# Attention loop of a hybrid encoder block on one Trainium2 core: transposes, mixture and scores of three different units placed together, the twelve projection products behind them

## Chip, cores, metric

One core of one Trainium2 chip. The time is that of one launch of the whole kernel in microseconds, the median of three runs. A profiled execution of the same kernel gives the trace.

## What is computed

The reference is one encoder layer on x (1, 512, 1024) in float32: a token mixer with two branches, a residual with layer norm, and a mixture of experts. Only the second branch of the mixer and the projections beside it matter here:

```python
q, k: (S, 8 heads, 2, 64)    v: (S, 8 heads, 128)
scores = q k^T / 8, masked to chunks of 64 tokens, for each head and each of its 2 parts
p = softmax(scores);  attn = p[part 0] - lam * p[part 1];  o = attn @ v
yb = rms_norm(o) * subln_g * (1 - lam_init)
merged = sigmoid(h @ w_gr) * (ya @ p_rnn) + sigmoid(h @ w_ga) * (yb @ p_attn)
mixer  = merged @ w_out
```

Afterwards 64 experts of width 256 are routed (8 of them per token), and each result row is scattered into a table `y_rows` in HBM that has been cleared to zero before.

## The kernel before, in words

The kernel is written engine by engine; each engine has its own program, in order, and they meet at semaphores. Each waits with `wait_ge`. TensorE (PE) multiplies and transposes, ScalarE (ACT) and VectorE (DVE) read the PSUM banks, GpSimd (POOL) does small things, SyncE (SP) issues DMAs.

**Units.** The attention stage walks over 32 units `u = 4 h + i`: head `h` (8) and block `i` (4) of 128 queries. Unit u sees `i + 1` key tiles of 128. Its steps are:
- `scores(u)` (L996, matmuls at L1007): eight recorded matmuls on 64x64 tiles into banks 2 and 3, or 4 and 5. It waits for the exponentials of u-2.
- `maxima(u)` (DVE, L1927 and L1929), the two exponentials (ACT, L1498), `combine(u)` (DVE, L1935 to L1940), which gives `attn`.
- `transpose_attn(u)` (L1011, L1018): i+1 transposes into bank 6, which ACT copies to `attn_t` (L1491). It waits for `attn` of u, for the copy of u-1, and, where u is the first unit of a head from head 2 on, at L1016 for `ybt_ready`, the semaphore of the head output (below), because that uses bank 6 too.
- `mix_values(u)` (L1021, L1031): `attn_t` times v, 2(i+1) recorded matmuls into bank 7, which DVE copies to `yb` (L1974).

**Heads.** When four units of a head are done, POOL squares `yb` (L734), DVE averages (`head_mean`, L1955), POOL takes the inverse root (L736), DVE scales (`head_norm`, L1961), PE transposes the four tiles into bank 6 (`transpose_head`, L1035, L1041), ACT reads bank 6 as `yb_t` (L1480, `ybt_ready`) and rounds it to `yb_hi` (L1482), DVE forms `yb_lo` (`head_low`, L1966).

**Products.** Beside the attention the stage computes the groups ("gr", h) and ("pr", h), 24 products each, twelve products to a unit: 128x128 weights times 128x512 data, in lines L900, L901 and L902 (the operands are split in a high and a low part, so each k takes three products). Weights arrive by DMA in blocks of two groups (L544), are rounded by ACT (`split_hi`, L1361) and the rest is formed by DVE (`split_lo`, L1745, `wlo_ready`); `begin` makes PE wait for that. Twice a head the bank is read: `gate_out` (ACT, L1417) and `merge_first` (DVE, L1950).

**The order** is written out by hand. PE in iteration u: scores(u), six products, transposes of u-1, six products, mixture of u-1, and at the first unit of a head from h = 2 on `transpose_head(h-2)`. One more iteration at the end serves unit 31, beside the 24 products of ("ga", 0). ACT in iteration u: copy of the transposes of u-1, exponentials of u, head output, weights. DVE: copy of the mixture of u-2, combine of u-1, maxima of u, then merge, weights, head steps.

**The zeros.** SP clears `y_rows` in eight transfers of 2 MB (L564) between the weight blocks, from `zeros`, a [128, 1024] tile written by POOL (L727).

Of the kernel before, what the change touches and what calls it, by code (L numbers as in the profile page):

```python
# [21 lines left out]
ACT = mybir.ActivationFunctionType  # L22
AX = mybir.AxisListType

P = 128
T = 512
D = 1024
NT = T // P
KD = D // P
NH = 8  # L30
# [91 lines left out]
def hybrid_block(nc, x, c, w_ada, b_ada, w_in, conv_w, conv_b, lru_w_a, lru_b_a, lru_w_i, lru_b_i, lru_lambda,  # L122
# [3 lines left out]
    with ctx:  # L126
# [74 lines left out]
        attn = [at(f"attn{p}", 198 + 2 * p, [P, T]) for p in range(2)]  # L201
        attn_t = at("attn_t", 202, [P, T])
        gate_s = at("gate_s", 206, [P, T])
# [95 lines left out]
        y_all = [at(f"y_all{s}", 38 + 16 * s, [P, TOPK // 2, D]) for s in range(4)]  # L299
        zeros = at("zeros", 170, [P, D])  # L300
        lane = at("lane", 201, [P, P])
# [213 lines left out]
        def _(sp):  # L515
# [22 lines left out]
            for n, (kind, b) in enumerate(BLOCKS):  # L538
# [20 lines left out]
                if kind in ("gr", "pr") and (kind, b) != ("gr", 0):  # L559

                    part = 2 * b + (kind == "pr")
                    sp.wait_ge(zeros_ready, 1)
                    for clear in ((0, 1) if part == 1 else (part,)):
                        sp.dma_start(y_rows[clear * T:(clear + 1) * T, :].rearrange("(j p) d -> p j d", p=P),  # L564
                                     bcast(zeros[:, :], 1, NT)).then_inc(rows_zeroed, 16)
                if (kind, b) == ("ga", 3):
# [274 lines left out]
        def _(pe):  # L841
# [179 lines left out]
            def mix_values(u):  # L1021
# [8 lines left out]
                for j in range(i + 1):  # L1030
                    last = nc.tensor.matmul(bank[7][:, 0:P], attn_t[:, j * P:(j + 1) * P], v_s[:, j, h * P:(h + 1) * P],  # L1031
                                            start=(j == 0), stop=(j == i))
                last.then_inc(mixed, 1)

            def transpose_head(h):  # L1035

                pe.wait_ge(yb_ready, h + 1)
                if h >= 1:
                    pe.wait_ge(ybt_ready, h)
                for t in range(NT):  # L1040
                    last = nc.tensor.transpose(bank[6][:, t * P:(t + 1) * P], yb[:, t, h * P:(h + 1) * P], ident[:, :])  # L1041
                last.then_inc(yb_tr, 1)

            for b in range(2):
                pe.wait_ge(main_read[b], 5 * KD // 2)
            for u in range(NT * NH + 1):
                h, i = u // NT, u % NT
                if u < NT * NH:
                    scores(u)
# [3 lines left out]
                    if u == 2:  # L1053
                        pe.wait_ge(yalo_ready, KD)
                    first, middle, end = (4 * (i % 2) + n for n in (0, 2, 4))
                    moving = (h_hi, h_lo) if i < 2 else (ya_hi, ya_lo)
                    channel_major(group, range(first, middle), *moving)
                else:
                    begin(("ga", 0))
                    channel_major(("ga", 0), range(KD // 2))  # L1060
                if u >= 1:
                    transpose_attn(u - 1)
                if u < NT * NH:
                    channel_major(group, range(middle, end), *moving)
                else:
                    channel_major(("ga", 0), range(KD // 2, KD))
                if u >= 1:
                    mix_values(u - 1)
                if u >= 2 * NT and i == 0:
                    transpose_head(h - 2)  # L1070

            begin(("pa", 0))
# [277 lines left out]
        def _(act):  # L1350
# [132 lines left out]

            for u in range(NT * NH + 1):
                h, i = u // NT, u % NT
                if u >= 1:
                    act.wait_ge(attn_tr, u)
                    if u >= 2:
                        act.wait_ge(mixed, u - 1)
                    w = ((u - 1) % NT + 1) * P  # L1490
                    nc.scalar.activation(attn_t[:, 0:w], bank[6][:, 0:w], ACT.Copy).then_inc(attn_t_ready, 1)  # L1491
                if u < NT * NH:
# [4 lines left out]
                    for k in range(2):  # L1497
                        nc.scalar.activation(prob[u % 2][k][:, 0:(i + 1) * P], bank[2 + 2 * (u % 2) + k][:, T - (i + 1) * P:T],  # L1498
                                             ACT.Exp, bias=unit_stats[:, u % 2, 2 + k:3 + k], scale=HC ** -0.5,
                                             accum_out=unit_stats[:, u % 2, 4 + k:5 + k]).then_inc(prob_ready, 1)  # L1500
                if u >= 2 * NT and i == 0:
                    head_out(h - 2)
# [169 lines left out]
        def _(dve):  # L1672
# [295 lines left out]

            for u in range(NT * NH + 2):
                h, i = u // NT, u % NT  # L1970
                if u >= 2:
                    ph, pi = (u - 2) // NT, (u - 2) % NT
                    dve.wait_ge(mixed, u - 1)
                    V.tensor_copy(yb[:, pi, ph * P:(ph + 1) * P], bank[7][:, 0:P]).then_inc(mixed_read, 1)  # L1974
                if 1 <= u <= NT * NH:
                    combine(u - 1)
                if u < NT * NH:
                    maxima(u)
                if i == 0 and h >= 1:
                    merge_first(h - 1)  # L1980
                if u == NT * NH:
                    split_lo(GROUP[("pa", 0)])
                if i == 1 and u < NT * NH:
                    split_lo(GROUP[("pr", h)])
                if i == 3 and u < NT * NH:
                    split_lo(GROUP[("gr", h)] + 2)
                if i == 1 and h >= 2:
                    head_low(h - 2)
                if i == 2 and h >= 1:
                    head_mean(h - 1)  # L1990
                if i == 3 and h >= 1:
                    head_norm(h - 1)

# [520 lines left out]
```

## Time and profile before

| | |
|---|---|
| median of 3 runs | 1302.7 us (1301.36 to 1304.47) |
| the profiled execution's own time | 1302.48 us |
| its span, first to last instruction | 1300.8 us |
| mean granted TensorE clock | 0.993 |
| PE busy | 1261.6 us (97%) |
| DVE busy | 837.4 us (64%) |
| ACT busy | 740.1 us (57%) |
| attention stage, first scores to last transposes | about 282 to 434 us |

Matmuls are pipelined, and a row shows one for longer than the distance to the next (a product takes 0.39 us in its row and the next begins 0.23 us later). So PE's busy share hides short waits, and what a step costs is read from the distance between starts. In a row of the timeline "x8" means that eight instructions of the same line follow each other; the row's second number is from the first's start to the last's end.

### The profile page before, as it was taken

Reading aid. Unit: us, or ns where it says so; the run is one execution under the profiler, and the core shown is the slowest. Engines: PE = TensorE matmul, PEld = TensorE weight load, DVE = VectorE, ACT = ScalarE, POOL = GpSimd, SP = SyncE. Lnnn points to the kernel's source line nnn. Section 1 sums busy time; section 2 is a strip of 40 time slices with the busy share of each in tenths; the row PEclk is TensorE's granted clock in tenths of the full one; section 3 lists DMA queues with packets and bytes.
Section 4 is the critical chain, followed back from the end, with each engine's and each line's share of the span. In section 5 each row is a group of like instructions: output and inputs, shape, how many; then the busy total and the mean of one; then the engine's idle time right before and its main releaser. Section 6 shows DMA issues by size and latency. Waiting matters only on the chain.

```text
span 1300.8 us, 22921 instructions
## 1 busy us (share of the span) xinstructions
PE 1261.6 (97%) x6367; PEld 725.4 (56%) x6367; DVE 837.4 (64%) x1771; ACT 740.1 (57%) x968; POOL 192.0 (15%) x373
## 2 busy tenths in 40 slices
PE   6999999999999999989999999999999999999995
PEld 6777788877777788865433333333333333333342
DVE  5837777667878555897455565555455555555578
ACT  4356452334554423113577777777677777777721
POOL 1000000000010100132122212221221221222100
PEclk9999999999999999999999999999999999999998
DMA  8832446669832551454789899999999999998396
GB/s 319 253 96 89 140 154 219 210 244 184 284 101 62 180 209 58 161 228 170 314 320 383 335 413 403 391 381 370 385 363 400 390 417 377 397 402 324 112 387 252
DMA packets 111603, 353.69 MB, mean 272 GB/s; under 512 B 20518, under 2 KB 59543, under 8 KB 85826
## 3 DMA queue, kind: packets, MB, share of 16 engines
q1 hardware_dynamic: 92642, 303.05, 63.6%
q0 software_dynamic: 18912, 50.01, 10.7%
q8 instruction: 28, 0.46, 0.2%
q14 instruction: 21, 0.17, 0.0%
HBM read 326.08 MB, written 47.21 MB: 287 GB/s over the span
## 4 chain that ended last, share of the span: by engine, by line
PE 79%; DVE 9%; DMA 7%; SPq 2%; issue 1%; ACT 1%; POOL 0%; ACTq 0%; DVEq 0%
PE bank L1244 25%; PE bank L1269 12%; PE bank L900 9%; PE bank L902 9%; PE bank L901 9%; DMA gu<-in_we_up 4%; PE bank L1231 3%; PE bank L1007 2%; PE bank L1254 2%; PE bank L1031 1%; DMA y_all<-y_rows 1%; PE bank L1133 1%; SPq L534 1%; DMA ada_first<-in_w_ada 1%; DVE x L2415 1%
## 5 line engine op out<-in xcount | busy, mean ns | idle before, releaser
L1244 PE MATMUL bank<-gu_use,x_t 128*64 128x512 f32 x1664 | 369.9, 597 | 0.0
L1595 ACT ACTIVATE gu_use<-gu 128x1024 f32 x208 | 209.1, 1058 | 57.3 <-PE bank L1244 32.4
L1244 PEld LDWEIGHTS bank<-gu_use,x_t 128*64 128x64 f32 x1664 | 115.2, 137 | 217.6 <-issue 217.4
L1588 ACT ACTIVATE down_use<-down 128x2048 f32 x103 | 190.9, 1901 | 0.0
L1269 PE MATMUL bank<-down_use,act_t 128*64 128x512 f32 x832 | 187.4, 592 | 0.0
L900 PE MATMUL bank<-h_hi,w_lo 128*128 128x512 f32 x432 | 173.9, 402 | 1.4 <-DVE w_lo L1745 1.4
L902 PE MATMUL bank<-h_hi,w_hi 128*128 128x512 f32 x432 | 168.7, 391 | 0.0
L2273 DVE COPY gu_use<-gu 128x1024 f32 x208 | 133.1, 691 | 55.3 <-PE bank L1244 41.8
L901 PE MATMUL bank<-h_lo,w_hi 128*128 128x512 f32 x432 | 168.4, 390 | 0.0
L1745 DVE TENSOR_TENSOR w_lo<-stream,w_hi 128x1024 fp32r<-128x1024 f32 x72 | 87.9, 1221 | 96.7 <-ACT w_hi L1361 96.6
L2239 DVE TENSOR_TENSOR pick<-slot_id,places 128x512 bf16<-128x512 f32 x53 | 36.7, 692 | 145.4 <-POOL columns L808 145.4
L1269 PEld LDWEIGHTS bank<-down_use,act_t 128*64 128x64 f32 x832 | 59.6, 137 | 119.0 <-issue 119.0
L787 POOL DMA_INDIRECT x_rows<-u_rows,row_index x52 | 53.6, 1032 | 434.5 <-DVE row_index L2251 252.4
L900 PEld LDWEIGHTS bank<-h_hi,w_lo 128*128 128x128 f32 x432 | 81.1, 188 | 28.1 <-issue 12.3
L1361 ACT ACTIVATE w_hi<-stream 128x1024 fp32r<-128x1024 f32 x72 | 75.9, 1055 | 32.1 <-PE bank L902 25.9
L902 PEld LDWEIGHTS bank<-h_hi,w_hi 128*128 128x128 f32 x432 | 81.1, 188 | 17.7
L901 PEld LDWEIGHTS bank<-h_lo,w_hi 128*128 128x128 f32 x432 | 81.2, 188 | 15.3
L2305 DVE TENSOR_TENSOR y_item<-bank,g_row 128x512 f32<-128x512 f32 x104 | 67.0, 686 | 2.9 <-PE bank L1269 2.1
L2251 DVE TENSOR_SCALAR row_index<-bank 64x1 int32<-64x1 f32 x104 | 23.4, 225 | 63.4 <-PE bank L1222 62.7
L1612 ACT ACTIVATE x_t<-bank 128x512 f32<-128x512 f32 x104 | 56.2, 598 | 4.1 <-PE bank L1231 4.1
L796 POOL DMA_INDIRECT y_rows<-y_item,y_index x50 | 50.2, 1005 | 43.4 <-issue 33.3
L1231 PE MATMUL bank<-ident,x_rows 128*128 128x128 f32 x416 | 55.8, 277 | 0.3 <-ACT x_t L1612 0.2
(345 smaller groups left out, 1721.6 us busy)
## 6 DMA issues: line engine op xcount, KB each, us to landing
gu<-in_we_gate SPq DMA_DIRECT2D x64, 1024.0 KB
gu<-in_we_up SPq DMA_DIRECT2D x64, 1024.0 KB
down<-in_we_down SPq DMA_DIRECT2D x64, 1024.0 KB
stream<-in_w_in SPq DMA_DIRECT2D x28, 1024.0 KB, 7.4
ada_w<-in_w_ada POOLq DMA_DIRECT2D x8, 2048.0 KB, 9.7
y_rows<-zeros SPq DMA_DIRECT2D x8, 2048.0 KB, 13.8
y_all<-y_rows SPq DMA_DIRECT2D x7, 2048.0 KB, 15.4
ada_first<-in_w_ada SPq DMA_DIRECT2D x16, 512.0 KB, 11.2
```

The source lines that it names most:

```text
L900: nc.tensor.matmul(o, w_lo[s][:, k, :], hi[:, k, :], start=(k == 0), stop=False)
L901: nc.tensor.matmul(o, w_hi[s][:, k, :], lo[:, k, :], start=False, stop=False)
L902: last = nc.tensor.matmul(o, w_hi[s][:, k, :], hi[:, k, :], start=False, stop=(k == KD - 1))
L1231: last = nc.tensor.transpose(bank[2 + k // 4][:, k % 4 * P:(k % 4 + 1) * P], x_rows[item.par][:, k * P:(k + 1) * P], ident[:, :])
L1244: last = nc.tensor.matmul(bank[item.par][rows, :], x_t[:, k, rows], gu_use[h][:, :, k, :], start=(k == 0), stop=(k == KD - 1))
L1269: last = nc.tensor.matmul(bank[5 + half][rows, :], act_t[:, f, rows], down_use[h][:, f, cols], start=(f == 0), stop=(f == FE - 1))
L1361: nc.scalar.activation(w_hi[n % 2][:, :, :], stream_of(group), ACT.Copy).then_inc(whi_ready, 1)
L1588: nc.scalar.activation(down_use[h][:, :, :], down[:, bass.ds(slot, 1), :, :].rearrange("p o k n -> p (o k) n"), ACT.Copy).then_inc(down_ta ...
L1595: return nc.scalar.activation(gu_use[h][:, 1, ks, :], gu[:, bass.ds(slot, 1), 1, ks, :].rearrange("p o k n -> p (o k) n"), ACT.Copy)
L1745: V.tensor_tensor(w_lo[n % 2][:, :, :], stream_of(group), w_hi[n % 2][:, :, :].bitcast(F32), ALU.subtract).then_inc(wlo_ready, 1)
L2273: return V.tensor_copy(gu_use[h][:, 0, ks, :], gu[:, bass.ds(slot, 1), 0, ks, :].rearrange("p o k n -> p (o k) n"))
L2305: last = V.tensor_tensor(y_item[item.par][:, cols], bank[5 + half][:, :], g2_row[:, cols], ALU.mult)
```

## The change

On PE, iteration u becomes: transposes of u-2, mixture of u-3, scores of u, all twelve products; then, at the second unit of a head, `transpose_head(h-2)`, with a new wait for the copies of the transposes before it. There are 34 iterations instead of 33, with the 24 products of ("ga", 0) shared out over the last two, and the mixture of unit 31 stands behind the loop. ACT and DVE follow: the copy is that of u-2, the head output moves to the second unit of the head, the `yb` copy is that of u-3 and comes after `combine(u-1)`, `head_low`, `head_mean` and `head_norm` move one unit on. `attn_t` gets a second buffer. It takes 2 KB of the place that `zeros` had, so `zeros` is [128, 512] now and each of the eight clearing transfers writes 2 KB runs instead of 4 KB runs, in another order of rows.

```diff
@@ -199,7 +199,7 @@
 
         prob = [[at(f"prob{p}{k}", 190 + 4 * p + 2 * k, [P, T]) for k in range(2)] for p in range(2)]
         attn = [at(f"attn{p}", 198 + 2 * p, [P, T]) for p in range(2)]
-        attn_t = at("attn_t", 202, [P, T])
+        attn_t = [at("attn_t0", 172, [P, T]), at("attn_t1", 202, [P, T])]
         gate_s = at("gate_s", 206, [P, T])
 
         branch = at("branch", 198, [P, T])
@@ -297,7 +297,7 @@
         shared_early = at("shared_early", 118, [P, FE, D])
 
         y_all = [at(f"y_all{s}", 38 + 16 * s, [P, TOPK // 2, D]) for s in range(4)]
-        zeros = at("zeros", 170, [P, D])
+        zeros = at("zeros", 170, [P, D // 2])
         lane = at("lane", 201, [P, P])
         tail_sums = at("tail_sums", 201.5625, [P, 2 * NT])
         passed = at("passed", 106, [P, D])
@@ -561,8 +561,8 @@
                     part = 2 * b + (kind == "pr")
                     sp.wait_ge(zeros_ready, 1)
                     for clear in ((0, 1) if part == 1 else (part,)):
-                        sp.dma_start(y_rows[clear * T:(clear + 1) * T, :].rearrange("(j p) d -> p j d", p=P),
-                                     bcast(zeros[:, :], 1, NT)).then_inc(rows_zeroed, 16)
+                        rows = y_rows[clear * T:(clear + 1) * T, :].rearrange("(p j) (c d) -> p (j c) d", p=P, c=2)
+                        sp.dma_start(rows, bcast(zeros[:, :], 1, 2 * NT)).then_inc(rows_zeroed, 16)
                 if (kind, b) == ("ga", 3):
 
                     sp.wait_ge(main_done, GROUP[("pr", KD - 1)] + 1)
@@ -1028,13 +1028,14 @@
                 else:
                     pe.wait_ge(ada_ready, 2)
                 for j in range(i + 1):
-                    last = nc.tensor.matmul(bank[7][:, 0:P], attn_t[:, j * P:(j + 1) * P], v_s[:, j, h * P:(h + 1) * P],
+                    last = nc.tensor.matmul(bank[7][:, 0:P], attn_t[u % 2][:, j * P:(j + 1) * P], v_s[:, j, h * P:(h + 1) * P],
                                             start=(j == 0), stop=(j == i))
                 last.then_inc(mixed, 1)
 
             def transpose_head(h):
 
                 pe.wait_ge(yb_ready, h + 1)
+                pe.wait_ge(attn_t_ready, min((h + 2) * NT, NT * NH))
                 if h >= 1:
                     pe.wait_ge(ybt_ready, h)
                 for t in range(NT):
@@ -1043,8 +1044,12 @@
 
             for b in range(2):
                 pe.wait_ge(main_read[b], 5 * KD // 2)
-            for u in range(NT * NH + 1):
+            for u in range(NT * NH + 2):
                 h, i = u // NT, u % NT
+                if u >= 2:
+                    transpose_attn(u - 2)
+                if u >= 3:
+                    mix_values(u - 3)
                 if u < NT * NH:
                     scores(u)
                     group = ("gr" if i < 2 else "pr", h)
@@ -1052,22 +1057,15 @@
                         begin(group)
                     if u == 2:
                         pe.wait_ge(yalo_ready, KD)
-                    first, middle, end = (4 * (i % 2) + n for n in (0, 2, 4))
                     moving = (h_hi, h_lo) if i < 2 else (ya_hi, ya_lo)
-                    channel_major(group, range(first, middle), *moving)
+                    channel_major(group, range(4 * (i % 2), 4 * (i % 2) + 4), *moving)
                 else:
-                    begin(("ga", 0))
-                    channel_major(("ga", 0), range(KD // 2))
-                if u >= 1:
-                    transpose_attn(u - 1)
-                if u < NT * NH:
-                    channel_major(group, range(middle, end), *moving)
-                else:
-                    channel_major(("ga", 0), range(KD // 2, KD))
-                if u >= 1:
-                    mix_values(u - 1)
-                if u >= 2 * NT and i == 0:
+                    if i == 0:
+                        begin(("ga", 0))
+                    channel_major(("ga", 0), range(4 * i, 4 * i + 4))
+                if h >= 2 and i == 1:
                     transpose_head(h - 2)
+            mix_values(NT * NH - 1)
 
             begin(("pa", 0))
             channel_major(("pa", 0), range(KD - 1), yb_hi, yb_lo)
@@ -1481,14 +1479,14 @@
                 act.wait_ge(ybt_ready, h + 1)
                 nc.scalar.activation(yb_hi[:, h, :], yb_t[:, h, :], ACT.Copy).then_inc(ybhi_ready, 1)
 
-            for u in range(NT * NH + 1):
+            for u in range(NT * NH + 2):
                 h, i = u // NT, u % NT
-                if u >= 1:
-                    act.wait_ge(attn_tr, u)
-                    if u >= 2:
-                        act.wait_ge(mixed, u - 1)
-                    w = ((u - 1) % NT + 1) * P
-                    nc.scalar.activation(attn_t[:, 0:w], bank[6][:, 0:w], ACT.Copy).then_inc(attn_t_ready, 1)
+                if u >= 2:
+                    act.wait_ge(attn_tr, u - 1)
+                    if u >= 4:
+                        act.wait_ge(mixed, u - 3)
+                    w = ((u - 2) % NT + 1) * P
+                    nc.scalar.activation(attn_t[u % 2][:, 0:w], bank[6][:, 0:w], ACT.Copy).then_inc(attn_t_ready, 1)
                 if u < NT * NH:
 
                     act.wait_ge(max_ready, u + 1)
@@ -1498,7 +1496,7 @@
                         nc.scalar.activation(prob[u % 2][k][:, 0:(i + 1) * P], bank[2 + 2 * (u % 2) + k][:, T - (i + 1) * P:T],
                                              ACT.Exp, bias=unit_stats[:, u % 2, 2 + k:3 + k], scale=HC ** -0.5,
                                              accum_out=unit_stats[:, u % 2, 4 + k:5 + k]).then_inc(prob_ready, 1)
-                if u >= 2 * NT and i == 0:
+                if h >= 2 and i == 1:
                     head_out(h - 2)
                 if u < NT * NH and i == (0 if h else 1):
                     split_hi(GROUP[("pr", h)])
@@ -1966,30 +1964,32 @@
                 V.tensor_tensor(yb_lo[:, h, :], yb_t[:, h, :], yb_hi[:, h, :].bitcast(F32), ALU.subtract
                                 ).then_inc(yblo_ready, 1)
 
-            for u in range(NT * NH + 2):
+            for u in range(NT * NH + 3):
                 h, i = u // NT, u % NT
-                if u >= 2:
-                    ph, pi = (u - 2) // NT, (u - 2) % NT
-                    dve.wait_ge(mixed, u - 1)
-                    V.tensor_copy(yb[:, pi, ph * P:(ph + 1) * P], bank[7][:, 0:P]).then_inc(mixed_read, 1)
                 if 1 <= u <= NT * NH:
                     combine(u - 1)
+                if u >= 3:
+                    ph, pi = (u - 3) // NT, (u - 3) % NT
+                    dve.wait_ge(mixed, u - 2)
+                    V.tensor_copy(yb[:, pi, ph * P:(ph + 1) * P], bank[7][:, 0:P]).then_inc(mixed_read, 1)
                 if u < NT * NH:
                     maxima(u)
-                if i == 0 and h >= 1:
+                if i == 0 and 1 <= h < NH:
                     merge_first(h - 1)
+                if u == NT * NH + 1:
+                    merge_first(NH - 1)
                 if u == NT * NH:
                     split_lo(GROUP[("pa", 0)])
                 if i == 1 and u < NT * NH:
                     split_lo(GROUP[("pr", h)])
                 if i == 3 and u < NT * NH:
                     split_lo(GROUP[("gr", h)] + 2)
-                if i == 1 and h >= 2:
+                if i == 2 and h >= 2:
                     head_low(h - 2)
-                if i == 2 and h >= 1:
+                if i == 3 and h >= 1:
                     head_mean(h - 1)
-                if i == 3 and h >= 1:
-                    head_norm(h - 1)
+                if i == 0 and h >= 2:
+                    head_norm(h - 2)
 
             def merged_low(k):
 
```

## Rows read from the trace of the kernel before

**Rows 1.** Chain of waits from 282 to 450 us, shares by line.
```profile
by line: PE bank L900 23.8%; PE bank L902 20.0%; PE bank L901 20.0%; PE bank L1007 12.9%; PE bank L1031 10.6%; PE bank L1018 6.1%; PE bank L1041 2.1%; issue 1.1%; DVE attn L1940 0.9%; DVE prob L1937 0.6%; DVE yb_lo L1966 0.4%; ACT yb_t L148
```
**Rows 2.** Busy time by stretch: PE, PEld, DVE, ACT, POOL busy (x count), clock, DMA share, GB/s.
```profile
282.00:446.00 164.00, 162.38 (x969) 119.20 (x969) 125.32 (x320) 78.83 (x204) 17.72 (x19) 1.00 0.64 162
```
**Rows 3.** Timeline of PE, 372 to 380 us: start us, us, engine, line, operation, tiles, count.
```profile
371.93 0.39 PE L902 MATMUL bank<-ya_hi,w_hi 128*128 128x512 f32 x1
372.17 0.49 PE L1018 MATMUL bank<-ident,attn 128*128 128x128 f32 x3
...
372.73 0.39 PE L901 MATMUL bank<-ya_lo,w_hi 128*128 128x512 f32 x1
...
373.89 0.83 PE L1031 MATMUL bank<-v_s,attn_t 128*128 128x128 f32 x6
374.65 0.45 PE L1007 MATMUL bank<-k_t,q_t 64*64 64x64 f32 x8
375.02 0.50 PE L900 MATMUL bank<-h_hi,w_lo 128*128 128x512 f32 x1
375.37 0.40 PE L901 MATMUL bank<-h_lo,w_hi 128*128 128x512 f32 x1
...
376.31 0.39 PE L902 MATMUL bank<-h_hi,w_hi 128*128 128x512 f32 x1
376.73 0.66 PE L1018 MATMUL bank<-ident,attn 128*128 128x128 f32 x4
...
377.46 0.40 PE L901 MATMUL bank<-h_lo,w_hi 128*128 128x512 f32 x1
...
378.60 1.05 PE L1031 MATMUL bank<-v_s,attn_t 128*128 128x128 f32 x8
379.49 0.60 PE L1041 MATMUL bank<-ident,yb 128*128 128x128 f32 x4
```
**Rows 4.** The same view, last transposes of the stage, where PE did not wait.
```profile
433.39 0.39 PE L902 MATMUL bank<-h_hi,w_hi 128*128 128x512 f32 x1
433.62 0.60 PE L1018 MATMUL bank<-ident,attn 128*128 128x128 f32 x4
...
434.29 0.40 PE L901 MATMUL bank<-h_lo,w_hi 128*128 128x512 f32 x1
```
**Rows 5.** Timeline of DVE, the end of combine that releases the transposes at 376.73.
```profile
375.92 0.75 DVE L1940 SCALAR_TENSOR_TENSOR attn<-prob,unit_stats,prob 128x512 f32<-128x512 f32 x1
```
**Rows 6.** Timeline of ACT, the head output read from bank 6, with the idle time before.
```profile
380.13 0.69 ACT L1480 ACTIVATE yb_t<-bank,subln 128x512 f32<-128x512 f32 x1 [1.41 <-PE bank L1041]
```
**Rows 7.** Timeline of ACT and DVE at the start of the stage, unit 1.
```profile
287.09 0.17 DVE L1929 TENSOR_SCALAR unit_stats<-unit_stats 128x2 f32<-128x2 f32 x1
...
287.98 0.28 ACT L1491 ACTIVATE attn_t<-bank 128x128 f32<-128x128 f32 x1 [3.12 <-PE bank L1018]
288.15 0.47 ACT L1498 ACTIVATE prob<-bank,unit_stats 128x256 f32<-128x256 f32 x1
...
289.05 1.06 ACT L1361 ACTIVATE w_hi<-stream 128x1024 fp32r<-128x1024 f32 x1
...
290.14 1.23 DVE L1745 TENSOR_TENSOR w_lo<-stream,w_hi 128x1024 fp32r<-128x1024 f32 x1 [2.88 <-ACT w_hi L1361]
```
**Rows 8.** Timeline of PE there: scores of unit 2 and the first product of ("pr", 0).
```profile
289.50 0.88 PE L1007 MATMUL bank<-k_t,q_t 64*64 64x320 f32 x8
291.47 0.47 PE L900 MATMUL bank<-ya_hi,w_lo 128*128 128x512 f32 x1 [1.10 <-issue]
```
**Rows 9.** The page's DMA issues, clearing of the table: count, size, us to landing.
```profile
y_rows<-zeros SPq DMA_DIRECT2D x8, 2048.0 KB, 13.8
```
**Rows 10.** The view of the tile `stream`: landing times of all weight blocks.
```profile
DMA to landing us min/median/max: 5.0/7.1/20.2
```
**Rows 11.** Timeline of SP, issue of the block ("pa", 0).
```profile
411.59 0.38 SPq L544 DMA_DIRECT2D stream<-in_p_attn  x1
```
**Rows 12.** Timeline of ACT, the first use of that block.
```profile
430.69 1.07 ACT L1361 ACTIVATE w_hi<-stream 128x1024 fp32r<-128x1024 f32 x1
```

## The prediction

> **What bounds the kernel now.** I read the chain of waits over the stage first: of the stretch from 282 to 450 us some 95% lie on PE's own lines, and the first others are an idle share without a releaser (1.1%) and the combine on DVE (0.9% and 0.6%) [rows 1]. Then the stretches: PE is busy for 162.38 of 164.00 us, DVE for 125.32, ACT for 78.83, POOL for 17.72, at a granted clock of 1.00, the level of 2.4 GHz [rows 2]. So PE sets the pace, and the reader is to see how little idle time there is to win: 1.6 us by this view. It hides short waits, since a product's row lasts 0.39 us though the next product starts after 0.23 us. For waits I therefore take distances between starts in PE's timeline. The stage behind (the projections of the second branch) is on the same engine, so what this stage gains or loses goes to the end one for one.
>
> **The order itself.** PE executes the same instructions after the change; what can change is what a neighbour costs. The pace of products alone is 0.23 us: five steps from 377.46 to 378.60 take 1.14 us [rows 3]. Around three transposes the distance from the product before (371.93) to the second product behind (372.73) is 0.80 us [rows 3]; less two product steps of 0.23 it is 0.34 us, 0.11 us a transpose. Around four, where PE didn't wait, it is 434.29 - 433.39 = 0.90 us [rows 4], less 0.46 it is 0.44 us, again 0.11 us each. Both points lie on a line through zero: going from products to transposes and back costs nothing beyond the transposes. A mixture runs at the same pace, six instructions in 0.76 us, and the scores follow it today as they will [rows 3]. What does cost is the step to the 64x64 tiles and back: 0.76 us for six mixture instructions is 0.10 more than 6 x 0.11, and the first product behind the scores lasts 375.37 - 375.02 = 0.35 us, 0.12 more than the pace [rows 3]. There is one such pair in a unit before and one after the change. I take **0 us** for the new neighbours. Transposes directly before a mixture do not occur in the trace; the nearest pair is the mixture of eight with the head's transposes behind it, 0.89 us to the next start, 0.11 each [rows 3], so again nothing. The ends: a gain of 0.12 us (a whole step) or a loss of 0.05 us in each of 32 units, that is 3.8 us less or 1.6 us more.
>
> The Trainium skill, "TensorEngine Tiling", section Key Properties, says that a change of tiling mode drains TensorE. The steps of 0.10 and 0.12 us agree with it, and since the change removes no such step, by that rule nothing is gained here; it speaks against this change.
>
> **The waits before four transposes go.** In the first unit of a head the twelve products are cut by the transposes of the unit before, four tiles wide, and these come too soon: combine ends at 375.92 + 0.75 = 376.67 [rows 5], the transposes start at 376.73, and the distance over them is 377.46 - 376.31 = 1.15 us [rows 3] where it is 0.90 without a wait [rows 4]. That is 0.25 us, in seven units of the stage (u = 4, 8, ... 28; two of them 0.02 us longer). With the transposes two units behind there is a whole unit of twelve products (2.8 us) more, so no wait is left: **-1.8 us**.
>
> **The wait at the start.** In unit 2 the scores start at 289.50 and the first product at 291.47, with 1.10 us of idle time before it [rows 8]. The product waits for the low part of the weights of ("pr", 0), done at 290.14 + 1.23 = 291.37 [rows 7]. Its chain hangs on PE: ACT copies the first transposes at 287.98, as they come in the middle of unit 1, then takes the exponentials (288.15), then rounds the weights (289.05) [rows 7]. Afterwards unit 1 has no transposes; the exponentials can start when the maxima are done, 287.09 + 0.17 = 287.26, so 0.86 us earlier, and so does all behind them. PE itself comes there only some 0.2 us earlier, since it has one transpose before the scores instead of a transpose and a mixture (0.3) and the step from them. So 1.1 - 0.86 + 0.2, or about 0.5 us of wait, are left: **-0.6 us**, with 0 and -1.1 as ends.
>
> **A new wait: bank 6.** `transpose_head` writes bank 6, and the transposes of a head's first unit may not start before ACT has read it (L1016). Now the scores of a unit and six products stand between the two, over 2 us, and nobody waits. After the change `transpose_head(h-2)` ends the second unit of head h, and the first instruction of the third is just this transposition (u-2 = 4h). Nothing stands between. From the start of the head's transposes (379.49) to the start of ACT's read (380.13) are 0.64 us, the read takes 0.69 [rows 3, 6], and a release reaches PE in 0.06 us (376.67 to 376.73). PE goes on 1.39 us after the start of four transposes that by themselves take 0.44. **0.95 us** are lost, in each of the heads h = 2 to 7 (the transposes of units 8, 12, ... 28), six times: **+5.7 us**. Queued behind it on PE are the mixture, the scores and twelve products, so nothing covers it; ACT and DVE only wait for PE. The loop's last `transpose_head` (u = 33) has no transposes behind it.
>
> **What else moves, at nothing.** DVE takes `combine` before the `yb` copy: bank 7 is asked for again one unit later, under twelve products. `head_low`, `head_mean`, `head_norm` keep their distances, one unit each. DVE's work is 125 us in 164 [rows 2], so it stays behind PE's pace with room. The new wait in `transpose_head` is for a copy made some 2 us earlier. At the end the mixture of unit 31 comes behind 24 products as before, now after `transpose_head(6)` and no longer before it; the steps to the last head's transposes keep 27 products as cover. SP: the clearing transfers keep their places, with twice as many runs of 2 KB. One takes 13.8 us to land now [rows 9]; weight blocks land after 7.1 us, at worst 20.2 [rows 10], and the shortest distance from issue to use among the blocks issued in the stage is 19.1 us (411.59 to 430.69) [rows 11, 12], for a block that has no clearing beside it. Cost 0, and up to 3 us if a block came late after all; cleared faster would gain nothing either. POOL's smaller memset has no one waiting at that time.
>
> **Sum**: -1.8 - 0.6 + 5.7 = +3.3 us. Against the profiled execution's own 1302.48 us (span 1300.8) this is 1305.8; it lies 0.2 under the median of the runs, and on the median of 1302.7 it gives **1306.0 us**. By the skill's rule alone the order gives nothing either, so its sum would be the same.
>
> **Rivals.**
> - *The order pays after all, faster.* If each of the two steps between products and other work that go away were worth what a step to or from small tiles is, 0.10 + 0.12 us over 32 units, 7.0 us, the time would be 1299.0. For it speaks only that such steps exist; the two points on the line through zero speak against. Chance 0.11.
> - *Bank 6 is hardly waited for.* Were ACT's read to start with the first transposes' end, or the wait covered by loads ahead, a third of the 5.7 would be left: 1302.2. Against it: ACT has nothing to do before this read and still starts 0.64 us after the first transpose [rows 3, 6]. 0.07.
> - *ACT comes late to bank 6, slower.* In the second unit ACT must finish the exponentials of that unit before the read. Before, it stood idle 1.41 us ahead of it [rows 6]. After, scores are followed by 2.8 us of products and then the head's transposes, while maxima and exponentials take about 2. If DVE is held by more than 1 us at that point, each further us costs six: at 1 us the time would be 1312. 0.09.
> - *The finer clearing delays a weight block* by up to 3 us: 1309. 0.04.
> - The order of the program is fixed by hand on each engine, so that the change doesn't do what it says I give no chance.
>
> **Numbers.** The forecast has 0.69. Its own range, from half of the start's gain, the bounds of the order (mostly the nearer ones) and the spread of the runs (3 us between lowest and highest, so about 1 for a median), is 1303.5 to 1308.2. No change from 1302.7 can be told within 0.2%, 2.6 us: from 1300.1 to 1305.3. Of the forecast's 0.69 some 0.23 lie under 1305.3. Slower: 0.46 + 0.09 + 0.04 = 0.59; same: 0.23 + 0.07 and 0.01 of the first rival, 0.31; faster: 0.10. The range from 1302.0 to 1309.0 leaves out the first rival and the late ACT, 0.20.
>
> **What will show it.** Right: in PE's timeline the distance from `transpose_head` (L1041) to the next transposes (L1018) is near 1.4 us in six places, with ACT's L1480 as releaser; the distance over four transposes, less the mixture, is at 0.11 each; the first product of ("pr", 0) waits about 0.5 us; a head takes 0.7 us longer than before. Wrong: heads that get shorter though this wait is there (the order pays), a distance near 0.5 us at L1041 (bank 6 not waited for), idle PE behind L1041 beyond 1 us with ACT still in L1498 (ACT late), or a w_hi on ACT that waits for a DMA.

## The result and the profile after

The changed kernel takes 1306.67 us (median of 20 runs, 1302.70 to 1313.63) against 1301.66 (20 runs, 1299.36 to 1307.19) for the kernel before on the same chips: ratio 1.0034, 95% interval 1.0022 to 1.0046, that is +4.4 us (2.9 to 6.0); the two medians by themselves differ by 5.0. It is slower, by a third of a per cent. The forecast was 1306.0 in a range of 1302.0 to 1309.0, with 0.59 on slower.

The runs of one kernel differ by up to 11 us here, so the mechanism is read from the traces. In the comparisons further down three runs of 1841, 2600 and 7306 us, far above all others, are left out of the ratios. I use one measure throughout, the **stage distance**: from the first scores to the last head's transposes on PE. Before it is 444.32 - 282.25 = 162.1 us, after it is 447.42 - 282.06 = 165.4: +3.3 us. The whole span grew by 2.8 (1303.6 for 1300.8).

The new wait, in the third unit of head 5, in PE's timeline of the changed kernel (the wait's idle time and its releaser in brackets):

```profile
382.85 0.60 PE L1042 MATMUL bank<-ident,yb 128*128 128x128 f32 x4
384.32 0.30 PE L1018 MATMUL bank<-ident,attn 128*128 128x128 f32 x1 [0.87 <-ACT yb_t L1478]
384.45 1.12 PE L1031 MATMUL bank<-v_s,attn_t 128*128 128x128 f32 x8
385.50 0.88 PE L1007 MATMUL bank<-k_t,q_t 64*64 64x320 f32 x8
```

and ACT beside it:

```profile
383.48 0.69 ACT L1478 ACTIVATE yb_t<-bank,subln 128x512 f32<-128x512 f32 x1 [1.36 <-PE bank L1042]
384.20 0.63 ACT L1480 ACTIVATE yb_hi<-yb_t 128x512 fp32r<-128x512 f32 x1
```

The head's transposes start at 382.85, ACT's read 0.63 later, it takes 0.69, and the next transposes start at 384.32: 1.47 us where four transposes by themselves take 0.44. All six places show 1.47. ACT had been idle for 1.36 us before the read, so it was ready. The view of the line of these transposes adds up the idle time before them (us, times) by what ended it:

```profile
  DVE attn L1938: 6.5, 6
  ACT yb_t L1478: 5.2, 6
```

The second line is PE's own, six times 0.87. The first belongs to the weight loads of the same six transposes, which the view puts down to the combine on DVE. That combine ends at 383.00 + 0.48 = 383.48, as the row below shows, 0.84 before PE goes on, and with 256 columns it is that of unit 21, not of the unit 20 that is transposed. ACT's read ends 0.15 before PE goes on. The run e5 below settles it.

```profile
383.00 0.48 DVE L1938 SCALAR_TENSOR_TENSOR attn<-prob,unit_stats,prob 128x256 f32<-128x256 f32 x1
```

In the chain of waits from 282 to 450 us ACT's read of bank 6 is now 2.9%, where [rows 1] had it last, behind an item of 0.4%; the combine on DVE, 0.9% there, is gone:

```profile
by line: PE bank L900 23.6%; PE bank L902 19.8%; PE bank L901 19.8%; PE bank L1007 13.4%; PE bank L1031 10.8%; PE bank L1018 5.9%; ACT yb_t L1478 2.9%; PE bank L1042 2.1%; issue 1.0%; DVE yb_lo L1964 0.4%; ACT yb_hi L1480 0.4%
```

The stretches show the idle PE too, 158.23 busy in 164 us for 162.38 in [rows 2], at the same granted clock of 1.00:

```profile
282.00:446.00 164.00, 158.23 (x953) 117.78 (x954) 123.01 (x317) 78.49 (x202) 17.10 (x16) 1.00 0.55 154
```

What went away is seen in the same timeline of PE. Four transposes now follow the products without a wait: 378.20 is 0.23 behind the last product, which is the pace, and the mixture starts 0.44 later, 0.11 a transpose. In [rows 3] the step from the last product to the four transposes was 376.73 - 376.31 = 0.42:

```profile
377.97 0.39 PE L902 MATMUL bank<-h_hi,w_hi 128*128 128x512 f32 x1
378.20 0.60 PE L1018 MATMUL bank<-ident,attn 128*128 128x128 f32 x4
...
378.64 0.83 PE L1031 MATMUL bank<-v_s,attn_t 128*128 128x128 f32 x6
379.40 0.66 PE L1007 MATMUL bank<-k_t,q_t 64*64 64x192 f32 x8
```

At the start of the stage the chain of [rows 7] runs earlier (timelines of DVE, ACT and PE). The exponentials no longer stand behind a copy and begin 0.03 us after the maxima's end. The first product of ("pr", 0) starts 1.36 us behind the scores' start, not 1.97 [rows 8]:

```profile
286.89 0.17 DVE L1927 TENSOR_SCALAR unit_stats<-unit_stats 128x2 f32<-128x2 f32 x1
...
287.09 0.48 ACT L1496 ACTIVATE prob<-bank,unit_stats 128x256 f32<-128x256 f32 x1 [2.41 <-DVE unit_stats L1927]
...
288.01 1.06 ACT L1359 ACTIVATE w_hi<-stream 128x1024 fp32r<-128x1024 f32 x1
...
289.06 0.88 PE L1007 MATMUL bank<-k_t,q_t 64*64 64x320 f32 x8
289.10 1.23 DVE L1743 TENSOR_TENSOR w_lo<-stream,w_hi 128x1024 fp32r<-128x1024 f32 x1 [2.04 <-ACT w_hi L1359]
...
290.42 0.47 PE L900 MATMUL bank<-ya_hi,w_lo 128*128 128x512 f32 x1 [0.49 <-issue]
```

The clearing transfers take 14.4 us to land instead of 13.8 [rows 9]; other traces of the same transfers give 13.4 to 14.6, so this is not a difference to build on. And no rounding of weights waits for a DMA in the stage:

```profile
y_rows<-zeros SPq DMA_DIRECT2D x8, 2048.0 KB, 14.4
```

### The profile page after: what moved, and what is told of

Same layout as the page of the kernel before. It is cut to its first block, busy times and chain, and to the rows that moved or that the text cites. A ratio compares the mean times of both kernels' runs of the same rounds, so it can differ in the third digit from the quotient of the medians.

```text
span 1303.6 us, 22921 instructions
## 1 busy us (share of the span) xinstructions
PE 1261.2 (97%) x6367; PEld 727.1 (56%) x6367; DVE 836.6 (64%) x1771; ACT 741.7 (57%) x968; POOL 191.8 (15%) x373
## 4 chain that ended last, share of the span: by engine, by line
PE 82%; DVE 8%; DMA 5%; ACT 2%; issue 1%; SPq 1%; POOL 0%; DVEq 0%; ACTq 0%
PE bank L1242 26%; PE bank L1267 13%; PE bank L900 10%; PE bank L902 9%; PE bank L901 9%; PE bank L1229 3%; DMA gu<-in_we_up 3%; PE bank L1007 2%; PE bank L1252 2%; PE bank L859 1%; PE bank L1031 1%; PE bank L1131 1%; DMA y_all<-y_rows 1%; DVE x L2415 1%; PE bank L1018 1%
## 5 line engine op out<-in xcount | busy, mean ns | idle before, releaser
L902 PE MATMUL bank<-h_hi,w_hi 128*128 128x512 f32 x432 | 168.6, 390 | 0.0
L901 PE MATMUL bank<-h_lo,w_hi 128*128 128x512 f32 x432 | 168.3, 390 | 0.0
L902 PEld LDWEIGHTS bank<-h_hi,w_hi 128*128 128x128 f32 x432 | 81.1, 188 | 17.4
L901 PEld LDWEIGHTS bank<-h_lo,w_hi 128*128 128x128 f32 x432 | 81.2, 188 | 15.8
L1496 ACT ACTIVATE prob<-bank,unit_stats 128x128 f32<-128x128 f32 (+3 forms) x64 | 33.3, 526 | 65.9 <-DVE unit_stats L1927 65.9
## 6 DMA issues: line engine op xcount, KB each, us to landing
y_rows<-zeros SPq DMA_DIRECT2D x8, 2048.0 KB, 14.4
```

Source lines behind the costliest of these rows:

```text
L901: nc.tensor.matmul(o, w_hi[s][:, k, :], lo[:, k, :], start=False, stop=False)
L902: last = nc.tensor.matmul(o, w_hi[s][:, k, :], hi[:, k, :], start=False, stop=(k == KD - 1))
```

## The experiments

Nine runs were made. Two take the wait away in different ways (e1, e2), one puts it alone into the kernel before (e3), one takes the clearing alone (e4), one stretches the wait (e5), one also removes the wait at the start (e6), and three repeat a kernel (e7, e8, e9). The table holds their stage distances, from PE's timeline of each, and ratios to the kernel before, run beside them on the same chip.

| kernel | first scores | last head's transposes | stage | ratio (95%) |
|---|---|---|---|---|
| before | 282.25 | 444.32 | 162.1 | 1 |
| changed | 282.06 | 447.42 | 165.4 | 1.0034 (1.0022 to 1.0046) |
| e1 head's transposes amid the products | 283.16 | 442.10 | 158.9 | 0.9977 (0.9958 to 0.9995) |
| e2 transposes behind the scores | 283.27 | 441.79 | 158.5 | 0.9957 (0.9938 to 0.9976) |
| e3 only the wait, in before | 283.32 | 451.60 | 168.3 | 1.0046 (1.0026 to 1.0065) |
| e4 only the clearing, in before | 283.13 | 445.17 | 162.0 | 0.9995 (0.9975 to 1.0016) |
| e5 bank read twice | 282.45 | 451.42 | 169.0 | one run, 1311.03 us |
| e6 e2 and weights earlier | 282.71 | 440.71 | 158.0 | 0.9976 (0.9959 to 0.9992) |
| e7 changed, again | 282.46 | 448.50 | 166.0 | 1.0022 (1.0006 to 1.0038) |
| e8 e2, again | 282.90 | 441.44 | 158.5 | 0.9984 (0.9968 to 1.0000) |
| e9 e6, again | 282.76 | 440.76 | 158.0 | 0.9970 (0.9953 to 0.9987) |

**e1: six products between the head's transposes and the next use of bank 6.** Against the changed kernel:

```diff
-                    channel_major(group, range(4 * (i % 2), 4 * (i % 2) + 4), *moving)
+                    if h >= 2 and i == 1:
+                        channel_major(group, range(4, 6), *moving)
+                        transpose_head(h - 2)
+                        channel_major(group, range(6, 8), *moving)
+                    else:
+                        channel_major(group, range(4 * (i % 2), 4 * (i % 2) + 4), *moving)
...
-                if h >= 2 and i == 1:
+                if u == NT * NH + 1:
                     transpose_head(h - 2)
```

> The changed kernel with one step moved: in the second unit of a head the head's transposes stand between the first six and the last six products of that unit, no longer behind all twelve. Stage distance is taken from the first scores to the last head's transposes: 162.1 us before the change (282.25 to 444.32), 165.4 after it (282.06 to 447.42). Theory (the wait for bank 6, six times 1.13 us from the distances 1.47 + 0.14 + 1.05 against 0.44 + 0.11 + 0.98, is the whole loss): the distance from the head's transposes to the next product is 0.4 us, the next transposes start without a wait, stage 158.6 to 159.2, and the kernel is faster than the one before by about 3 us, ratio 0.997 to 0.998. Rival (the new grouping or the finer clearing costs time by itself): the stage stays above 162 and the ratio at or above 1.000.

PE's timeline of e1, head 5 (lines L901 and L902 left out between):

```profile
379.39 0.60 PE L1042 MATMUL bank<-ident,yb 128*128 128x128 f32 x4
379.74 0.48 PE L900 MATMUL bank<-h_hi,w_lo 128*128 128x512 f32 x1
...
381.21 0.28 PE L1018 MATMUL bank<-ident,attn 128*128 128x128 f32 x1
381.33 1.05 PE L1031 MATMUL bank<-v_s,attn_t 128*128 128x128 f32 x8
382.31 0.88 PE L1007 MATMUL bank<-k_t,q_t 64*64 64x320 f32 x8
```

The next product starts 0.35 us behind the head's transposes, the next transposes have no idle time before them, and the transposes and the mixture together are 0.08 us shorter than behind the wait (0.12 + 0.98 for 0.13 + 1.05). The stage is 6.4 us shorter than the changed one with the same steps, 3.1 us shorter than before, the ratio below 1. The wait is the whole loss; the rival that the grouping itself costs time is out.

The same trace shows where the grouping gains. Within a run of products the steps get shorter behind the sixth: here 383.46 to 384.62 are five steps of 0.232 us, 384.62 to 385.75 five of 0.226.

```profile
383.12 0.50 PE L900 MATMUL bank<-ya_hi,w_lo 128*128 128x512 f32 x1
383.46 0.39 PE L901 MATMUL bank<-ya_lo,w_hi 128*128 128x512 f32 x1
...
384.62 0.39 PE L900 MATMUL bank<-ya_hi,w_lo 128*128 128x512 f32 x1
...
385.75 0.39 PE L902 MATMUL bank<-ya_hi,w_hi 128*128 128x512 f32 x1
```

The kernel before has this too, in its one long run, the 27 products ahead of the last head's transposes: five steps of 0.232 from 438.39 to 439.55, and fifteen of 0.227 from 440.69 to 444.09.

```profile
438.39 0.40 PE L901 MATMUL bank<-yb_lo,w_hi 128*128 128x512 f32 x1
...
439.55 0.39 PE L900 MATMUL bank<-yb_hi,w_lo 128*128 128x512 f32 x1
...
440.69 0.39 PE L902 MATMUL bank<-yb_hi,w_hi 128*128 128x512 f32 x1
...
444.09 0.39 PE L902 MATMUL bank<-h_hi,w_hi 128*128 128x512 f32 x1
```

But nearly all its runs are of six products. Over the stage the steps from product to product below 0.29 us, which leaves out the first of a run and waits, have a mean of 0.2318 us before (303 steps) and 0.2298 in e1 (353 steps): 0.7 us in all. What makes them shorter no run shows.

**e2: the mixture and the scores between them.** Against the changed kernel:

```diff
+                late = h >= 2 and i == 2
-                if u >= 2:
+                if u >= 2 and not late:
                     transpose_attn(u - 2)
...
                     scores(u)
+                    if late:
+                        transpose_attn(u - 2)
```

> The changed kernel with another step moved: in the third unit of heads 2 to 7 the transposes come behind the mixture and the scores instead of ahead of them, so that 0.98 + 0.81 us of work stand between the head's transposes and the next use of bank 6. Theory of the wait: the read by ScalarE (ready 1.47 us after the head's transposes start, 1.03 us after they would end) is covered, stage 158.6 to 159.5, with one more step from small tiles to whole tiles of 0.1 us in each of the six; ratio 0.997 to 0.998. Rival (any transposes near the head's transposes cost time, whoever reads the bank): the same 1.1 us a head stay, stage 165, ratio 1.003.

```profile
380.65 0.60 PE L1042 MATMUL bank<-ident,yb 128*128 128x128 f32 x4
381.08 1.06 PE L1031 MATMUL bank<-v_s,attn_t 128*128 128x128 f32 x8
382.07 0.88 PE L1007 MATMUL bank<-k_t,q_t 64*64 64x320 f32 x8
382.88 0.33 PE L1018 MATMUL bank<-ident,attn 128*128 128x128 f32 x1
382.96 0.48 PE L900 MATMUL bank<-ya_hi,w_lo 128*128 128x512 f32 x1
```

The wait is covered by mixture and scores, the stage 158.5 us. The extra step from small tiles that I had allowed for, 0.1 us in each of the six units, did not come: there is one such step in the unit in either order, and the stage is 0.4 us shorter than that of e1. The ratio 0.9957 is lower than the stage gives, 158.5 - 162.1 = -3.6 us or 0.9972; this I tried again (e8).

**e3: nothing but the wait, in the kernel before.** Against the kernel before (the same moves on ACT ahead of its copy, and `head_low` one unit later on DVE):

```diff
+                if h >= 2 and i == 1:
+                    transpose_head(h - 2)
                 if u >= 1:
                     transpose_attn(u - 1)
...
-                if u >= 2 * NT and i == 0:
+                if u == NT * NH:
                     transpose_head(h - 2)
```

> The kernel before the change with nothing but the wait: for heads 2 to 7 the head's transposes stand directly ahead of the transposes of the head's first unit, in the middle of the second unit's products, and ScalarE reads the head out ahead of its copy (the low part on VectorE one unit later). Everything else as before, attn_t with one buffer, the order transposes / six products / mixture as before. Theory: six waits of 1.0 to 1.15 us, stage 162.1 + 6.0 to 6.9 = 168.1 to 169.0, ratio about 1.005. Rival (the loss belongs to the new grouping, not to this neighbourhood): stage 162 to 163, ratio 1.000.

```profile
385.95 0.60 PE L1041 MATMUL bank<-ident,yb 128*128 128x128 f32 x4
387.42 0.30 PE L1018 MATMUL bank<-ident,attn 128*128 128x128 f32 x1 [0.87 <-ACT yb_t L1482]
387.48 0.48 PE L900 MATMUL bank<-h_hi,w_lo 128*128 128x512 f32 x1
```

All six places show the same 1.47 us and the same releaser, with the old order and one buffer of `attn_t`. Stage +6.2 us in six places, 1.03 each, ratio 1.0046. The neighbourhood alone makes the wait.

**e4: the finer clearing alone**, in the kernel before: `zeros` of 128x512 and the transfer of the change.

```diff
-        zeros = at("zeros", 170, [P, D])
+        zeros = at("zeros", 170, [P, D // 2])
...
+                        rows = y_rows[clear * T:(clear + 1) * T, :].rearrange("(p j) (c d) -> p (j c) d", p=P, c=2)
+                        sp.dma_start(rows, bcast(zeros[:, :], 1, 2 * NT)).then_inc(rows_zeroed, 16)
```

> The kernel before with the finer clearing alone: zeros of 128x512, eight transfers of 2 KB runs in the new order of rows. Measured for the whole change are 4.4 us (ratio 1.0034) where its stage is 3.3 us longer. Theory: the clearing costs nothing, stage 162.1, ratio 1.000 within 0.001; the 1.1 us between are noise of the runs. Rival: the clearing, or the order in which the table's rows were written, costs the missing 1 us, in the stage or later, ratio 1.001.

The stage is 162.0 us and the ratio 0.9995, with an interval of 0.2% to either side. So there is no cost in the stage; a cost of 1 us behind it can be neither seen nor excluded by the interval alone.

**e5: a longer read.** In the changed kernel `yb_hi` too is made from bank 6, ahead of `yb_t` (and DVE's `head_low` gets a wait for `yb_t` besides, not shown):

```diff
-                nc.scalar.activation(yb_t[:, h, :], bank[6][:, :], ACT.Copy, scale=subln[:, 0:1]).then_inc(ybt_ready, 1)
-                act.wait_ge(ybt_ready, h + 1)
-                nc.scalar.activation(yb_hi[:, h, :], yb_t[:, h, :], ACT.Copy).then_inc(ybhi_ready, 1)
+                nc.scalar.activation(yb_hi[:, h, :], bank[6][:, :], ACT.Copy, scale=subln[:, 0:1]).then_inc(ybhi_ready, 1)
+                nc.scalar.activation(yb_t[:, h, :], bank[6][:, :], ACT.Copy, scale=subln[:, 0:1]).then_inc(ybt_ready, 1)
```

> The changed kernel with ScalarE's part of the wait made longer: the rounded head (yb_hi) is made from bank 6 too, ahead of yb_t, so that the bank is read twice, about 0.69 and 0.69 us, and released only after the second. ScalarE's work as a whole stays the same. Theory (TensorE waits for the end of ScalarE's read): the distance from the head's transposes to the next ones grows from 1.47 to 2.0 to 2.2 us in six places, stage 165.4 + 3.3 to 4.3 = 168.7 to 169.7. Rival (the 1.47 us are a fixed cost of two different transposes in a row on one bank, or the wait ends at something else): the distance stays 1.47, stage 165.4.

The mixed timeline of e5:

```profile
385.06 0.60 PE L1042 MATMUL bank<-ident,yb 128*128 128x128 f32 x4
385.69 0.69 ACT L1478 ACTIVATE yb_hi<-bank,subln 128x512 fp32r<-128x512 f32 x1 [1.36 <-PE bank L1042]
386.28 0.68 ACT L1479 ACTIVATE yb_t<-bank,subln 128x512 f32<-128x512 f32 x1
387.10 0.30 PE L1018 MATMUL bank<-ident,attn 128*128 128x128 f32 x1 [1.45 <-ACT yb_t L1479]
```

The distance is 2.04 us in all six places, 0.57 more; the second read starts 0.59 behind the first. The stage is 3.6 us longer than that of the changed kernel. PE goes on 0.14 us behind the end of ACT's last read here and 0.15 there, so it waits for that end: neither a fixed cost of two neighbours on one bank nor the combine on DVE would have moved with it.

**e6: the wait at the start.** e2 with one more edit on ACT:

```diff
-                if u < NT * NH and i == (0 if h else 1):
+                if u < NT * NH and i == 0:
                     split_hi(GROUP[("pr", h)])
```

> The kernel of e2_t_late (transposes behind mixture and scores in the third unit of heads 2 to 7) and, besides, the rounding of the weights of (pr, 0) on ScalarE one unit earlier, as in the other heads. It is there for the wait that is left at the start: scores of unit 2 to the first product 1.36 us, of which 0.81 are the scores. Theory: these weights are the last thing there, the distance falls to 0.8, stage 158.5 - 0.5 = 158.0, ratio 0.995 to 0.996. Rival (the products wait there for the rounded branch on VectorE or for the weights' DMA): the distance stays 1.36, stage 158.5.

```profile
289.70 0.88 PE L1007 MATMUL bank<-k_t,q_t 64*64 64x320 f32 x8
290.50 0.50 PE L900 MATMUL bank<-ya_hi,w_lo 128*128 128x512 f32 x1
```

The first product now starts 0.80 us behind the scores' start and PE has no idle time before it: the weights' rounding was the last thing it waited for there. The stage is 158.0 us, 0.5 less than that of e2.

**e7: the changed kernel again.**

> The changed kernel as it is, once more, beside the two above on the same chip. Its stage was 3.3 us longer than before the change, its ratio 1.0034 (4.4 us, interval 2.9 to 6.0). Theory: the stage is the whole difference, ratio 1.0025 with an interval that holds it, stage 165.4 again. Rival: something behind the stage costs 1 us more: the ratio is again 1.0034 or above and the stretch from the last head's transposes to the end is longer than before by about 1 us.

The ratio is 1.0022, with an interval that holds the 1.0025 of the stage and also 1.0034. In five of six places the distance is 1.47 us; in the first it is 2.23, because ACT's read started 1.40 us behind the transposes, with its exponentials done at 324.04 (timelines of PE and ACT):

```profile
323.84 0.20 ACT L1496 ACTIVATION_READ_ACCUMULATOR prob<-bank,unit_stats 128x1 f32 x1
...
324.76 0.60 PE L1042 MATMUL bank<-ident,yb 128*128 128x128 f32 x4
326.16 0.69 ACT L1478 ACTIVATE yb_t<-bank,subln 128x512 f32<-128x512 f32 x1 [2.12 <-PE bank L1042]
```

That makes the stage 166.0. The execution that was profiled here was also the longest of the twelve, 1311.02 us. What delayed ACT's read by 0.76 us the profile does not show; it stays open, and it happened once in the 18 such places of the three traces with this wait (changed, e3, e7). The stretch behind the stage, span less last head's transposes, was 856.2 us in the first trace of this kernel and 860.8 in this one. Over all traces it lies between 853.6 (e1) and 860.8, with 856.5 before, and e2 and e8, one and the same kernel, have 858.3 and 860.6. So a 1 us effect behind the stage is not shown, nor excluded.

**e8 and e9: e2 and e6 again**, side by side.

> The kernel of e2_t_late once more, beside e9. Its stage was 158.5 us and its ratio 0.9957 (0.9938 to 0.9976), more than the 3.6 us of the stage give (0.9972). Theory (the stage is all): stage 158.5, ratio near 0.997, an interval that holds 0.9972. Rival (transposes behind the scores help somewhere else too): ratio again below 0.996.

> The kernel of e6_late_and_early_weights once more, on the same chip as e8. Stage 158.0, so 0.5 us under e8. Theory: its ratio is that of e8 less 0.0004, which the runs can't tell apart from e8; both lie below 0.999. Rival (rounding the weights earlier costs as much later): ratio above that of e8 by 0.001 or more, though the stage is shorter.

Stages 158.5 and 158.0 as before. e8's ratio is 0.9984, with an interval that holds 0.9972, as the interval of e2 does; so the 0.9957 of e2 needs no cause beyond the scatter of its runs. e9 has 0.9970, e6 0.9976. Earlier weights cost nothing later that could be seen. The version of e6 and e9 beats both kernels: 1299.6 and 1299.8 us (medians), about 3 to 4 us under the kernel before, as its stage says (162.1 - 158.0 = 4.1).

## Why the prediction was right, point by point

- **What bounds**: PE, in the stage as a whole. Every edit that changed PE's distances changed the stage by about as much: e3 +6.2 for six waits of 1.03, e5 +3.6 for six of 0.57, e6 -0.5 for 0.56.
- **The order costs nothing**: nearly. Transposes before a mixture, which the trace of before had not, take 0.11 us each. But the term is not zero. e1 is 3.1 us under the kernel before, of which the waits before four transposes and the wait at the start make 1.75 + 0.6. The remaining 0.8 us, 0.02 in a unit, are the shorter steps in the longer runs of products (0.7 by the means under e1). I had taken 0.23 for every product and looked only at what stands beside a run, not at its length. The gain lies between my ends (-3.8 and +1.6), near the zero I took. The first rival, a gain of 7.0 us, is out. The tile steps are still there once in a unit: in e1 the mixture of eight takes 0.98 us to the scores, 0.10 more than 8 x 0.11, and the first product behind the scores 0.34, 0.11 more than the pace. That agrees with the rule of the Trainium skill ("TensorEngine Tiling (Array Packing)", Key Properties) that a change of tiling mode drains TensorE, and with its consequence that this change could not win them.
- **The waits before four transposes go, -1.8 us**: right, 0.25 in seven units; in PE's timeline of the changed kernel none of them is left.
- **The wait at the start, -0.6 us**: right. 1.97 became 1.36, and e6 showed that the weights' rounding on ACT is what it waits for.
- **Bank 6, +5.7 us**: mechanism, six places and releaser right; the size was 0.7 too small. I gave the release 0.06 us, from DVE to PE [rows 5, 3]. From ACT to PE it is 384.32 - (383.48 + 0.69) = 0.15. And behind the wait the transposes and the mixture of eight take 0.13 + 1.05 instead of 0.12 + 0.98. Measured by e1 the wait costs 6.4 us, 1.07 a head; I had 0.95.
- **What else moves, at nothing**: right for the stage (e4), and no weights were late. The clearing took 0.6 us longer to land in the first trace of the changed kernel, but that is scatter: over the nine traces with 2 KB runs it is 13.4 to 14.6.
- **The sum, +3.3**: the stage says +3.3, and that it fits so closely is luck: two errors cancel in it, 0.7 too little on the wait and 0.8 too little on the gains. The ratio of the first comparison gives +4.4 us, that of the second (e7) +2.9; both intervals hold 3.3, the first only just. That the forecast of 1306.0 came within 0.7 of the measured 1306.67 is in part luck too, since the kernel before came out at 1301.66 in 20 runs where I had started from 1302.7.
- **Rivals**: bank 6 hardly waited for, out by the six distances. ACT late at bank 6: once, 0.76 us, in e7, and not by the cause I had named, since its exponentials were done at 324.04, 0.72 before the head's transposes even started. The clearing: out in the stage.

## What to carry to other kernels

When steps are regrouped on the engine that sets the pace, follow each PSUM bank and not only each engine: a bank that two uses share needs the writer's last result, the reader's start and its whole read between them, here 1.0 us beyond the work, and what stood between them before was its cover. Read what a neighbour costs from two counts of the same step (three and four transposes): a line through zero says that there is no switching cost to win. It does not say that the pace of the work beside it is the same in a short and in a long run; that has to be read by itself. And a wait can be moved under work that is there anyway; the change became a gain as soon as the mixture and the scores, or six products, stood between the two uses.

## What the runs showed of the hardware beyond what I had expected

- A release from ACT reached PE's next transposes 0.15 us after the end of ACT's row (0.14 to 0.15 in all six places of the changed kernel, of e3 and of e5), one from DVE in 0.06 us [rows 5, 3].
- In a run of 128x512 products the steps fall from 0.232 us to 0.227 behind the sixth or so (e1, and the run of 27 before), at a granted clock of 1.00.
- Two activations of 128x512 from the same bank in a row start 0.59 us apart, though each row lasts 0.69 (e5).
- Eight mixture instructions take 0.98 us behind running products and 1.05 behind an idle PE, at a granted clock of 1.00 in both (e1 against the changed kernel).
- A 2 MB clearing transfer in runs of 2 KB landed after 13.4 to 14.6 us (medians of the nine traces that have them; e4 13.8) and in runs of 4 KB after 13.8 (before and e3). Twice as many runs made no difference that can be told from the scatter.
